# Two decoder stacks on one core: the scan's inverse turned instead of multiplied twice, and the order at chained ends

## The reference

```python
# first block, per layer
x = x + 0.5 * swiglu(rms_norm(x, g1), w_gate, w_up, w_down)      # D_FF = 2816
x = x + hybrid_mixer(rms_norm(x, g), ...)
x = x + 0.5 * swiglu(rms_norm(x, g2), w_gate, w_up, w_down)
# second block, per layer
p = rmsnorm(x, norm1_g) @ w_in
y_rw = rwkv7_branch(...)      # per head: S_t = S_{t-1}(diag(w_t) - kk_t^T (a_t kk_t)) + v_t^T k_t
proj = einsum('bsgc,gcd->bsgd', stack([y_rw, y_ret, y_sg], 2), w_branch)
x = x + sum(sigmoid(gate_logits) * proj, axis=2) @ w_out
x = x + conv_ffn(rmsnorm(x, norm2_g), w_up, conv_w, conv_b, w_down)
```

## Time and profile before

| | |
|---|---|
| median of 3 runs | 2283.04 us (2278.32 to 2289.6) |
| the execution profiled | 2291.36 us |
| span of its trace | 2289.6 us, 39101 instructions |
| PE busy | 2189.4 us |
| DVE busy | 1409.1 us |
| ACT busy | 1002.0 us |
| mean granted clock of PE | 0.98 |
| read from memory | 346.0 MB |

### The profile page before, as it was taken

The page is one execution under the profiler, slowest core; times in us unless marked ns, Lnnn a source line. Parts: engine busy times, 40 slices in busy tenths (PEclk is TensorE's granted clock), DMA queues, the critical chain, the costliest instruction groups (busy, mean ns, idle before and its releaser), DMA issues. The chain is left out here.

```text
span 2289.6 us, 39101 instructions
## 1 busy us (share of the span) xinstructions
PE 2189.4 (96%) x16210; PEld 2049.0 (89%) x16210; DVE 1409.1 (62%) x2091; ACT 1002.0 (44%) x1409; POOL 18.8 (1%) x18
## 2 busy tenths in 40 slices
PE   7999999999999999999999899899999989989998
PEld 7999987999999997899889799889988979988997
DVE  6555366655744656755575766576767576657775
ACT  4434266433533445633364333355445433335443
POOL 0000000000000000000000100000000010000000
PEclk9999899999999999999999899999999989999999
DMA  8435332553554522544443223365534322336551
GB/s 306 191 144 192 122 121 93 221 212 148 200 207 169 191 93 84 200 188 164 165 158 111 79 84 103 99 248 196 184 114 164 106 80 87 102 94 247 203 184 47
DMA packets 79579, 349.08 MB, mean 152 GB/s; under 512 B 21200, under 2 KB 30544, under 8 KB 45520
## 3 DMA queue, kind: packets, MB, share of 16 engines
q1 hardware_dynamic: 79440, 347.07, 42.0%
HBM read 345.99 MB, written 1.05 MB: 152 GB/s over the span
## 5 line engine op out<-in xcount | busy, mean ns | idle before, releaser
L89 PE MATMUL bank<-ffn_hT_split,n_split_gate_up 128*128 128x256 f32 x1408 | 392.0, 278 | 2.8 <-DVE ffn_hT_split L192 2.4
L90 PE MATMUL bank<-ffn_hT_split,n_split_gate_up 128*128 128x256 f32 x1408 | 391.9, 278 | 0.0
L91 PE MATMUL bank<-ffn_hT_split,n_split_gate_up 128*128 128x256 f32 x1408 | 391.4, 278 | 0.0
L89 PEld LDWEIGHTS bank<-ffn_hT_split,n_split_gate_up 128*128 128x128 f32 x1408 | 265.6, 189 | 5.3 <-issue 3.6
L90 PEld LDWEIGHTS bank<-ffn_hT_split,n_split_gate_up 128*128 128x128 f32 x1408 | 265.6, 189 | 1.5
L91 PEld LDWEIGHTS bank<-ffn_hT_split,n_split_gate_up 128*128 128x128 f32 x1408 | 265.1, 188 | 0.0
L1787 DVE TENSOR_TENSOR mix_parts<-mix_arrived,mix_parts 128x1024 fp32r<-128x1024 f32 x88 | 107.4, 1224 | 137.5 <-ACT mix_parts L1782 137.2
L356 ACT ACTIVATE work<-bank 128x256 f32<-128x256 f32 x88 | 33.2, 382 | 314.9 <-PE bank L91 314.7
L454 DVE TENSOR_TENSOR work<-bank,work 128x256 f32<-128x256 f32 x88 | 37.2, 423 | 197.0 <-ACT work L356 197.0
L435 DVE TENSOR_TENSOR ffn_split_down<-ffn_arrived_down,ffn_split_down 128x2048 fp32r<-128x2048 f32 x44 | 100.8, 2291 | 85.4 <-ACT ffn_split_down L351 85.4
L417 DVE TENSOR_TENSOR n_split_gate_up<-arrived_gate_up,n_split_gate_up 128x2048 fp32r<-128x2048 f32 x64 | 144.7, 2287 | 12.5 <-ACT n_split_gate_up L341 12.5
(11 more groups left out here) (383 smaller groups left out, 6160.7 us busy)
## 6 DMA issues: line engine op xcount, KB each, us to landing
arrived_gate_up<-in_ffn SPq DMA_DIRECT2D x64, 1024.0 KB, 8.6
ffn_arrived_down<-in_ffn SPq DMA_DIRECT2D x44, 1024.0 KB, 4.9
mix_arrived<-in_mix_w SPq DMA_DIRECT2D x88, 512.0 KB, 3.6
rrived_gate_up<-in_conv_ffn SPq DMA_DIRECT2D x32, 1024.0 KB, 6.9
_arrived_gate_up<-in_ffn SPq DMA_DIRECT2D x24, 1024.0 KB, 6.7
mixer_arrived<-in_w_in SPq DMA_DIRECT2D x22, 1024.0 KB, 6.8
onv_ffn_arrived_down<-in_conv_ffn SPq DMA_DIRECT2D x22, 1024.0 KB, 4.8
irst_project_arrived<-in_w_in SPq DMA_DIRECT2D x17, 1024.0 KB, 4.9
```

The costliest lines, as they stand in the source:

```text
L89: pe.matmul(out, lhs[0], rhs[0], start=start, stop=False)
L90: pe.matmul(out, lhs[0], rhs[1], start=False, stop=False)
L91: return pe.matmul(out, lhs[1], rhs[0], start=False, stop=stop)
```

## The change

It has five parts.

1. **Inverse.** `inverse_T` is no longer multiplied and added. Two steps after a quad of `inverse` is updated, PE turns its four units (`turn_inverse`, four transposes) into bank 6 or 7, and ACT copies them to `inverse_T` (`copy_inverse`). `outer_product(n)` waits for the copy of step n - 4.
2. **Order ahead of and in the loop.** Pieces 2 and 3 are run by PE behind `score(1, 1)` and `score(1, 2)`; steps 0 to 3 have none. The last two steps of the loop have none either: the tail begins at piece 22 (`TAIL`) and holds ten pieces where it held eight. On DVE `keep(0, 1)` goes ahead of the norm of the spatial branch.
3. **Order in the tail.** On DVE `scale(1)` goes ahead of `turned_low(0)`; five pieces instead of three stand between the last rows product and branch 0.
4. **Chained ends.** Behind both mixers DVE adds tile 0's residual first, then makes the next phase's gate low, then tile 0's norm. In every chained feed-forward the up weights are split later: ACT's high part behind tile 0's norm, DVE's low part behind the four lows of `hT_split`.
5. **Buffers.** Columns of the first block's and the convolutional feed-forward's buffers, of the units and of the inverse's rows are moved; no wait is changed for it.

```diff
@@ ffn_phase, scalar
         if ph.prev:
             ph.prev.free_parts(act)
-            high_gu(0, 0, 16, False)
+            high_part(0, 0, 16, False, 0)
...
         for t in range(NT):
             norm_scalar(act, c, ph, t, ph.prev or ph.start)
+            if ph.prev and t == 0:
+                high_part(0, 0, 16, False, 1)
@@ ffn_phase, vector_split and vector
     def vector_split(dve):
-        for part in range(2):
-            low_part(dve, 0, 0, part)
+        low_part(dve, 0, 0, 0)
...
         if ph.prev:
             turned_low_vector(dve, c, turn_banks, ph, hT[0], hT[1])
+            low_part(dve, 0, 0, 1)
@@ nsa_phase and scan_mix_phase, end of vector
-        ph.nxt.vector_split(dve)
         for t in range(NT):
...
+            if t == 0:
+                ph.nxt.vector_split(dve)
             ph.nxt.vector_norm(dve, t)
@@ second_map
-    c.conv_ffn = FfnMemory(at, "conv_ffn", dict(hT=18576, act=40600, arrived=(blocks(8192, 2), blocks(26264, 2)), arrived_down=12288,
-                                                parts=(blocks(0, 2, 2), ((36504, 38552), (24216, 34456))),
-                                                down_parts=((14480, 16528), (30360, 32408)), taps=22672))
+    c.conv_ffn = FfnMemory(at, "conv_ffn", dict(hT=18656, act=30432, arrived=(blocks(8240, 2), blocks(26320, 2)), arrived_down=12368,
+                                                parts=(blocks(48, 2, 2), ((36656, 38704), (24240, 40752))),
+                                                down_parts=((14512, 16560), (32560, 34608)), taps=22752))
@@ scan_mix_phase
-    AT_STEP = {0: 2, 1: 3, **{n: n for n in range(4, TOTAL)}}
+    TAIL = FIRST_GATE0 - 2
+    AT_STEP = {0: 2, 1: 3, **{n: n for n in range(4, TAIL)}}
@@ scalar
+        def copy_inverse(n):
+            act.wait_ge(s["x_turned"], n + 1)
+            act.activation(quad(x, n % QUADS), bank4(6 + n % 2), ACT.Copy).then_inc(s["x_copied"], 1)
...
+            if 2 <= n < BOTH + 2:
+                copy_inverse(n - 2)
@@ vector
         decay(3)
+        keep(0, 1)
...
-        keep(0, 1)
...
-            if n < BOTH:
-                dve.tensor_tensor(quad(x, q), quad(x, q), bank4(6 + n % 2), ALU.add).then_inc(s["updated"], 1)
...
+        scale(1)
+        after(TAIL + 6)
         turned_low(0)
-        scale(1)
@@ tensor
         score(1, 1)
+        piece(2)
         score(1, 2)
+        piece(3)
         score(1, 3)
...
             if n >= 2:
-                pe.wait_ge(s["updated"], n_updates(n - 2))
+                pe.wait_ge(s["updated"], n - 1)
+            if n >= QUADS:
+                pe.wait_ge(s["x_copied"], n - QUADS + 1)
...
-            if n < BOTH:
-                for i in range(4):
-                    last = pe.matmul(c.ps[6 + n % 2][:, i * P:(i + 1) * P], inner[:, n % 2, i * P:(i + 1) * P],
-                                     x[:, 4 * q + i], start=True, stop=True)
             last.then_inc(s["outer_ready"], 1)
+
+        def turn_inverse(n):
+            pe.wait_ge(s["updated"], n + 1)
+            if n >= 2:
+                pe.wait_ge(s["x_copied"], n - 1)
+            for i in range(4):
+                last = pe.transpose(c.ps[6 + n % 2][:, i * P:(i + 1) * P], z[:, 4 * (n % QUADS) + i], c.ident)
+            last.then_inc(s["x_turned"], 1)
...
+            if 2 <= n < BOTH + 2:
+                turn_inverse(n - 2)
...
-            if n in AT_STEP:
+            if n in AT_STEP and n >= QUADS:
                 piece(AT_STEP[n])
```

More of the change, by code:

```diff
@@ L1739, in second_map @@
     c.rhs0 = at("rw_rhs", LOCAL + 9216, [P, RW_W])
[L1740 to L1745 removed]
+    c.z = at("inverse", 37584, [P, UNITS, P])[:]
+    c.low = at("level_rows", 39632, [P, 2, 512])
+    c.a_rows = at("a_rows", 34512, [P, UNITS, P])[:]
+    c.y_parts = at("branches_T", 26320, [P, 2, 2, 4, S], F32R)
+    c.half_arrived = [at(f"mix_arrived{n}", col, [P, HALF_UNIT])[:] for n, col in enumerate((40752, 41776, 36560))]
+    c.half_parts = [at(f"mix_parts{n}", col, [P, 2, HALF_UNIT], F32R) for n, col in enumerate((30416, 32464, 24272))]
     c.y_rw_parts = at("rw_T_parts", 7208, [P, 2, 4, S], F32R)
     c.merged_parts = at("merged_parts", LOCAL, [P, 2, KT, S], F32R)
[L1748 to L1750 removed]
+    c.conv_ffn = FfnMemory(at, "conv_ffn", dict(hT=18656, act=30432, arrived=(blocks(8240, 2), blocks(26320, 2)), arrived_down=12368,
+                                                parts=(blocks(48, 2, 2), ((36656, 38704), (24240, 40752))),
+                                                down_parts=((14512, 16560), (32560, 34608)), taps=22752))
 R_, K_, V_, A_, LW, KK, BH, KH, KR, KR2, E1, E2 = range(12)
@@ L2342, in scalar @@
         root(0)
-        after(FIRST_GATE0 + 4)
+        after(TAIL + 4)
         square(1)
         root(1)
-        after(FIRST_GATE0 + 5)
+        after(TAIL + 5)
+        after(TAIL + 6)
         turned_high(0)
-        after(FIRST_GATE0 + 6)
-        after(FIRST_GATE0 + 7)
+        after(TAIL + 7)
+        after(TAIL + 8)
         turned_high(1)
+        after(TAIL + 9)
         def merged_high(p):
@@ L2817, in w_product @@
             last.then_inc(s["w_ready"], 1)
-        piece(FIRST_GATE0)
+        piece(TAIL)
         pe.wait_ge(s["inner_copied"], TOTAL)
         w_product(0)
-        piece(FIRST_GATE0 + 1)
+        piece(TAIL + 1)
         pe.wait_ge(s["w_copied"], 1)
@@ L2840, in tensor @@
                       start=(u == NH), stop=False, skip_group_check=True)
-        piece(FIRST_GATE0 + 2)
+        piece(TAIL + 2)
         pe.wait_ge(s["state_copied"], 1)
@@ L2849, in tensor @@
                       start=False, stop=False, skip_group_check=True)
-        piece(FIRST_GATE0 + 3)
+        piece(TAIL + 3)
         w_product(1)
-        piece(FIRST_GATE0 + 4)
+        piece(TAIL + 4)
         pe.wait_ge(s["w_copied"], 2)
@@ L2857, in tensor @@
         last.then_inc(s["y_ready"], 1)
-        piece(FIRST_GATE0 + 5)
+        piece(TAIL + 5)
+        piece(TAIL + 6)
         def turn_y(t):
@@ L2866, in tensor @@
         turn_y(0)
-        piece(FIRST_GATE0 + 6)
-        piece(FIRST_GATE0 + 7)
+        piece(TAIL + 7)
+        piece(TAIL + 8)
         turn_y(1)
+        piece(TAIL + 9)
         for m in range(FIRST_BR0, N_HALF_UNITS - RING):
```

59 lines of the change are left out of this document (26 added, 33 removed).

## The result

The changed kernel takes 2207.39 us (median of 4 runs, 2206.2 to 2210.58) against 2283.07 us (4 runs, 2278.32 to 2289.6): a ratio of 0.9669, 95% interval 0.9643 to 0.9695, 75.7 us less. I had forecast 49.7 less, 2233 us, and 2214 to 2256 as the range. The direction was right; the time lies 7 us under the range.

The account below looks back on a forecast made before the run. PE was taken to bound the kernel, busy 2189.4 of 2289.6 us. The terms, 2 x (10.2 + 6.3 + 4.1) + 5.7 + 3.5 - 0.7 = 49.7 us off the median 2283.0, gave 2233 us, range 2214 to 2256.

Parts of the forecast that it names:

- Buffers: Moved buffer columns in all places: no wait or shape changes, so priced at 0.
- Transposes: Scan steps: four transposes replace four products, saving PE 9.0 us per layer, 2.7 in the first four steps, 6.3 after.
- Steps of 5.1 us: Scan loop: sign that each step takes 5.1 us, from 5.54 before, with `inverse` transposes of 0.44.
- Ahead of the loop: Stretch up to step 4's inner product: reordering and full clock gain 10.2 us per layer, 6.3 of it clock.
- the forecast's case: The clock holds ahead of the loop and the whole sum is gained, 2233 us; chance 0.62.
- its rival's: Clock falls all the same ahead of the loop and in the tail: gain only 34 us, 2249 us; chance 0.20.
- no clock of 0.5 between the first decay and step 4: Ahead of the loop: sign that PE never drops to the 1.2 GHz level there.
- Tail: Behind the loop: two pieces more fill waits, gaining 4.1 us per layer, ends 1.0 and 5.
- The wait "near 2": Tail: sign of one wait near 2 us, worked out as 1.95 ahead of piece 4.
- Chained ends: Behind the mixers: 5.7 us gained in the first block, 3.5 in the second, less 0.7 for the up low.
- The late up low: All five chained ends: up low ends about 0.15 us behind PE's 24 gate matmuls, costing 0.7 us together.
- the rivals: Clock falls, 2249 us (0.20); only removed work counts, 2266 (0.11); transposed inverse late, about 2283 (0.04); loop at 1.2 GHz (0.03).

Follow-up runs that it names:

- old_places: The changed kernel with the buffer columns of the kernel before, everything else kept: 2230.39 us, ratio 0.9761 to the kernel before.
- inverse_only: The kernel before with only the transposed inverse made by four transposes and a copy, not products and an addition: 2270.49 us, ratio 0.9939.
- order_only: The kernel before with only the new order of pieces, tail, and earlier masked copies and scalings: 2255.66 us, ratio 0.9875.
- ends_only: The kernel before with only the new order at the chained ends (norm ahead, up weights' split last): 2274.8 us, ratio 0.9963.

## Why the prediction was wrong, and where it was right

**Buffers: the step that failed.** "I price it 0 from both sides", I wrote, because DVE's low split takes 2.29 us at either place. That row bounds what a place costs VectorE. The engine that reads the moved buffers most is PE, and for it I had no bound; the trace of before had one in plain view, two slots of one buffer whose hidden products took 117.8 and 113.4 ns a matmul. The term measured 21 to 23 us: 22.8 alone, 21 to 23.0 taken away. The spans of `old_places` and of the changed kernel differ by 22.4 us. Lined up by stage, from the first hidden product to the last down product, the six feed-forwards give 2.6, 2.5, 1.7, 3.5, 5.7 and 4.9 of them, 21.0 in all, and each scan loop 1.1 (91.3 us and 90.2 from step 4's inner product to inner product 23). The spacings account for this. In a plain feed-forward of `old_places` 4 to 6 chunks x 96 x 4.3 ns are 1.7 to 2.5 us and 264 down products x 4.5 ns 1.2 us, 2.9 to 3.7 together; in a convolutional one all the chunks are slow, some 5.9. Of that go up to 0.8 us in each of the three stages whose chunks 0 and 1 ran at 117.8 in the changed kernel. The other stages differ by up to 1.8 us to either side, and nearly cancel.

**All else: right in the main, and 3 to 5 us short.** Without the buffers the change gives 2230.39 us, where I said 2233. Its parts are off by more than its sum, so that the sum comes this close is partly luck. I line up the traces by stage. One of these stages is the stretch ahead of the loop, from score 2 to step 4's inner product, which in the changed kernel stands between these two lines of PE's timeline:

```profile
1242.38 1.13 PE L2724 MATMUL bank<-rw_kept 64*128 64x256 f32 x8
...
1283.50 1.06 PE L2790 MATMUL bank<-inverse,level_rows 128*128 128x128 f32 x8
```

- *Transposes.* Steps of 5.1 us were forecast; `inverse_only` has them (from 1874.22 to 1879.32 us in its chain, 5.10), and from step 4's inner product to inner product 23 its layers take 91.3 us where they took 97.6, the 6.3 of my sum. Ahead of step 4 they gain 1.9 and 3.5 us for 2.7. The medians show 12.9 us of these 18.0. No product waits for ACT's copy of the transposed inverse. The rule that spoke against it (the Trainium skill, TensorE: Matmul & The Clock Gate, Part 4, about 275 ns for a transpose in a kernel) would by my estimate have made this a loss of some 8 us, 18.0 less 26; here the 160 transposes take 0.44 us for four, 110 ns each, and the measurement decides. A record of one lasts 273 ns, since it overlaps with the next. A product costs two such records, a transpose one, and that is the gain.
- *Ahead of the loop.* The waits were forecast as 7.3 us a layer and are 4.8: 0.95, 1.3, 1.1, 0.6 and 0.9 where I had 1.45, 1.65, 1.35, 1.05 and 1.45. My walk along DVE's queue found each wait and its order and made each some 0.4 us too long. But PE's work in the stretch was mis-sized the other way. From score 2, its wait included, to step 4's inner product the changed kernel takes 41.2 us (the two lines above, and 0.1 for the wait). Of these 36.3 are work, where I had 34.8. The gain is 11.3 us for 10.2, and in `old_places` 22.9 for 20.4 in both layers. The clock held from score 2 on, the forecast's case (0.62) and not its rival's (0.20). By the letter of my sign, "no clock of 0.5 between the first decay and step 4", it didn't: the 3.4 us at 1233.5 overlap the first decay. They cost at most half of PE's 2.95 us in them, and neither `old_places` nor the kernel before has them.
- *Tail.* The wait "near 2" is 2.13, the third branch's is 0.73 in layer 0 and 1.31 in layer 1 (0.9), outer product 23's 0.86 (1.2). No fall of the clock came behind the 2.13, to which I had given a half. From inner product 23 to the feed-forward's first product `order_only` gains 4.1 and 5.2 us, where I had 4.1. In `old_places` the same stretch, now with the chained end, gains 13.5 in both layers for 11.7.
- *Chained ends.* 8.6 us for 8.5. In the first block L162 waits 0.16 us where it had 0.81, and no longer 2.1; from the last down product of one feed-forward to the first product behind the mixer `ends_only` takes 3.2 us less than `order_only`, which keeps the old ends, for 2.85. In the second block the first wait falls from 1.48 and 2.10 to 0.3, and tile 1 waits 0.8 in both layers. The late up low, to which I gave 0.7 us, shows as no wait in the profile.

Of the rivals none came true. The range failed because I let only the terms vary that I had priced; a part of the diff with a price of 0 "from both sides" put nothing into it.

## What to carry to other kernels

When a diff moves buffers that TensorE reads, compute for each pair of operands the start of the stationary one less the start of the moving one, modulo 256 bytes, and look up in the trace what spacing (start to start, not the duration printed) pairs at that distance have; two slots of a ring that the same code reads at two spacings are the sign to look for. Leave out the first chunks of a stage, which here had either spacing at either distance. And expect no fixed gain: the mixer's pieces at distance 64 had 117.8 ns and more. Price a part of a change from rows of the engine that it touches, and let a part without such a row widen the range. Where an order removes waits, do the walk along the queue, but take the parts apart on the chip, and line up the traces by stage: here a stretch came out within about 1 us only because its waits were forecast 2.4 us too long and its work 1.5 us too short, and the term that failed outright was the one thought free.

## What the runs showed of the hardware

- The spacing of fp32r matmuls in a full stream depends on the distance of their two operands in memory: 113.3 to 120.0 ns with 256 moving columns in the feed-forwards, 226.7 to 233.8 ns with 512. The Trainium skill (TensorE: Matmul & The Clock Gate, Part 2, on the steps of a matmul) says that TensorE has two independent read ports, one for the streamed operand and one for the weights. Taken strictly that would leave no room for what is seen here: with all else equal, the place of the loaded operand against the streamed one costs up to 6%. The mechanism was not found, only the distance on which it turns.
- At the best distance for 256 columns a stage runs at one of two spacings, 113.6 or 117.8 ns, differently from one execution to the next of one program; the place makes it possible and does not force it. The two lie 4.5 ns apart with 256 columns (113.3 and 117.8 within a set) and 4.6 with 512 at distance 192 (228.8 and 233.4, in the first down products): a fixed amount for a matmul, not a share of it.
- The best distance differs between the two kinds: 64 bytes with 256 columns, 0 or 192 with 512 (226.7 to 229.9 ns), where 64 is among the worst (233.0 to 233.5).
- Four fp32 transposes of 128x128 take 0.44 us in the loop, half of four products, and the clock stays at 1.00 through twenty steps with them (1280 to 1379 us).
